# Reordering the first layer norm and the split of the feed-forward weights, signalling the selected rows in halves, and issuing fewer unread products, in a two-block transformer kernel on one core

## The reference

```python
logits = (h @ router_w + router_b)
top_v, top_i = lax.top_k(logits, TOP_K)            # 4 of 32
gates = jax.nn.softmax(top_v, axis=-1)
hid = xb @ w1[e] + b1[e]                           # rows chosen for expert e, 1024 -> 2048
y = clamped_swiglu(hid[:, :1024], hid[:, 1024:]) @ w2[e] + b2[e]
x = x + gf * segment_sum(y * gate)
x = rmsnorm(x, final_norm_w)                       # end of the first block
```

```python
h = layer_norm(2 ** 0.25 * x + mix @ w_out, ln1_g, ln1_b)
h = layer_norm(2 ** 0.25 * h + square(relu(h @ w_ff1)) @ w_ff2, ln2_g, ln2_b)
out = h + sigmoid(h @ w_ple_gate + b) * (p @ w_ple)
```

## Time and profile before

| | before |
|---|---|
| median of 3 runs (lowest, highest) | 1504.31 us (1504.18, 1506.39) |
| the profiled execution | 1501.75 us, span of the trace 1500.0 us |
| TensorE products busy | 1380.5 us (92%) |
| VectorE, ScalarE, GpSimd busy | 503.1, 311.3, 45.3 us |
| mean granted clock of TensorE | 0.981 |
| loaded | 500.01 MB, 333 GB/s over the span |

### The profile page before, as it was taken

The page is one execution under the profiler, slowest core; times in us unless marked ns, Lnnn a source line. Parts: engine busy times, 40 slices in busy tenths (PEclk is TensorE's granted clock), DMA queues, the critical chain, the costliest instruction groups (busy, mean ns, idle before and its releaser), DMA issues.

```text
span 1500.0 us, 17452 instructions
## 1 busy us (share of the span) xinstructions
PE 1380.5 (92%) x6836; PEld 747.5 (50%) x6836; DVE 503.1 (34%) x898; ACT 311.3 (21%) x454; POOL 45.3 (3%) x70
## 2 busy tenths in 40 slices
PE   5998999999989899999898998998999899899998
PEld 2884456433434324334333343243343487789987
DVE  2846435113113112121131131121111546755566
ACT  3515233101101101001011011010010453444451
POOL 2000002100000000000000000000000111000000
PEclk9999999999999999999999999999999999999999
DMA  9319906999999999999999999999999762465640
GB/s 388 117 52 368 415 4 221 412 428 428 428 428 430 428 429 429 429 428 429 429 428 428 430 428 429 428 429 428 429 429 428 320 224 74 153 184 182 195 141 29
DMA packets 61898, 500.01 MB, mean 333 GB/s; under 512 B 5192, under 2 KB 21864, under 8 KB 34144
## 3 DMA queue, kind: packets, MB, share of 16 engines
q1 hardware_dynamic: 59616, 492.85, 79.8%
q0 software_dynamic: 2032, 6.05, 1.3%
q10 hardware_dynamic: 208, 0.54, 0.1%
HBM read 498.37 MB, written 1.05 MB: 333 GB/s over the span
## 4 chain that ended last, share of the span: by engine, by line
PE 65%; DMA 22%; DVE 7%; issue 3%; ACT 1%; SPq 1%; DVEq 0%; ACTq 0%; PEldq 0%
PE bank L1553 27%; DMA ring<-in_w 20%; PE bank L635 17%; PE bank L673 15%; PE bank L693 2%; DMA ring<-in_w_in 2%; DVE dk L748 1%; DVE mrows L752 1%; DVE dk L742 1%; PE bank L681 1%; PE bank L655 1%; SPq L539 1%; PE bank L646 1%; SPq L592 0%; PE bank L1740 0%
## 5 line engine op out<-in xcount | busy, mean ns | idle before, releaser
L635 PE MATMUL bank<-ring,xn 128*64 128x512 f32 x2048 | 467.6, 610 | 66.2 <-DMA ring<-in_w 64.7
L635 PEld LDWEIGHTS bank<-ring,xn 128*64 128x64 f32 x2048 | 163.5, 140 | 360.2 <-issue 360.2
L673 PE MATMUL bank<-ring,dq 128*64 128x512 f32 x1024 | 226.8, 595 | 0.0
L737 DVE TENSOR_SCALAR mrows<-bank 128x512 f32<-128x512 f32 x32 | 20.6, 686 | 477.5 <-PE bank L635 477.5
L707 ACT ACTIVATE sq<-mrows 128x512 f32<-128x512 f32 x32 | 19.6, 630 | 774.5 <-DVE mrows L737 774.5
L673 PEld LDWEIGHTS bank<-ring,dq 128*64 128x64 f32 x1024 | 70.6, 137 | 136.5 <-issue 133.8
L761 DVE TENSOR_TENSOR dk<-bank,bc 128x512 f32<-128x512 f32 x32 | 22.1, 692 | 236.2 <-PE bank L673 236.2
L494 DVE TENSOR_TENSOR w_lo<-ring,w_hi 128x2048 fp32r<-128x2048 f32 x34 | 77.7, 2291 | 31.8 <-ACT w_hi L489 31.7
L1553 PE MATMUL bank<-x_hi,w_hi 128*128 128x256 f32 x256 | 73.2, 286 | 1.8 <-DVE h_lo L1434 1.8
L1553 PE MATMUL bank<-h_lo,w_hi 128*128 128x256 f32 x256 | 73.1, 285 | 0.0
L1553 PE MATMUL bank<-x_hi,w_lo 128*128 128x256 f32 x256 | 73.1, 285 | 0.0
(11 more groups left out here) (413 smaller groups left out, 1516.1 us busy)
## 6 DMA issues: line engine op xcount, KB each, us to landing
ring<-in_w SPq DMA_DIRECT2D x192, 2048.0 KB, 17.1
ring<-in_w_ff SPq DMA_DIRECT2D x32, 1024.0 KB, 5.5
ring<-in_w_ada SPq DMA_DIRECT2D x24, 1024.0 KB, 16.6
ring<-in_w_out SPq DMA_DIRECT2D x8, 1024.0 KB, 10.2
ring<-in_w_in SPq DMA_DIRECT2D x8, 992.0 KB, 25.2
ring<-in_w_in SPq DMA_DIRECT2D x8, 640.0 KB, 11.3
ring<-in_w_ple_gate SPq DMA_DIRECT2D x4, 1024.0 KB, 4.8
xc<-in_ctx SPq DMA_DIRECT2D x1, 1024.0 KB, 5.0
```

The costliest lines, as they stand in the source:

```text
L635: m = pe.matmul(banks[bank_no][mine(i), :], gathered[:, k, mine(i)], rows_of(at + i, 2)[:, k % 2, q * 512:(q + 1) * 512], start=k == 0, st ...
L673: m = pe.matmul(banks[OUT_BANKS[c]][mine(i), :], actT[:, k, mine(i)], rows_of(8 + 2 * j + i, 4)[:, r, c * 512:(c + 1) * 512], start=k == 0 ...
L737: dve.tensor_scalar(gs[:, half * 512:half * 512 + 512], banks[GATE_BANKS[half]][:], LIMIT, None, ALU.min)\
```

## The change

It does four things. In the diff the lines that begin with @@ name the function or the engine's program.

- `gather` signals `xt_full` after each half (k = 3 and k = 7), `gather_out` waits for and signals each half, and `hidden` waits for the first half at k = 0 and for the second at k = 4. The other waits count in halves.
- The two `keep_running` around the rank products have 1 and 2 products instead of 3 and 4.
- In the final norm of the first block ScalarE takes the root of tile 0 ahead of the squares of tile 1.
- Around the first layer norm: the first feed-forward chunk is rounded and subtracted ahead of the norm of tile 0; VectorE norms tile 1 directly behind tile 0 and takes the four low parts of `h1T` behind both; ScalarE takes root 1 ahead of the copies of the embedding banks, of which the last stands behind the roundings of tile 1; TensorE has the transposes of tile 1 ahead of the fourth embedding bank, and claims the banks of the sums behind `wide_part(0)`.

```diff
@@ gather, hidden
-            m.then_inc(moe("xt_full", which), 1)
+                if k % 4 == 3:
+                    m.then_inc(moe("xt_full", which), 1)
 
         def hidden(pe, n, which):
 
-            pe.wait_ge(moe("xt_read", which), n + 1)
             for k in range(KD):
                 at = k // 2 * 2
+                if k % 4 == 0:
+                    pe.wait_ge(moe("xt_read", which), n * 2 + (k // 4 + 1))
...
@@ pe_rest
-            pe.wait_ge(moe("xt_read", which), n + (1 + ahead))
+            pe.wait_ge(moe("xt_read", which), n * 2 + (2 + 2 * ahead))
...
@@ gather_out
-            act.wait_ge(moe("xt_full", which), n + 1)
             for j in range(2):
-                m = act.activation(gathered[:, 4 * j:4 * j + 4, :],
-                                   banks[GATHER_BANKS[j]][:].rearrange("p (k s) -> p k s", k=4), ACT.Copy)
-            m.then_inc(moe("xt_read", which), 1)
+                act.wait_ge(moe("xt_full", which), n * 2 + (j + 1))
+                act.activation(gathered[:, 4 * j:4 * j + 4, :],
+                               banks[GATHER_BANKS[j]][:].rearrange("p (k s) -> p k s", k=4), ACT.Copy)\
+                    .then_inc(moe("xt_read", which), 1)
...
@@ scalar: final norm of the first block
             for t in range(NT):
                 act.wait_ge(moe("y_added", MAIN), 4 * PAIRS - 1 + 2 * t)
                 step(act.activation(xn[:, 1, :], x2[:, t, :], ACT.Square, accum_out=stat[:, t:t + 1]), "ss3_done")
-            for t in range(NT):
                 act.wait_ge(sem("ms_done"), 6 + t)
                 step(act.activation(stat[:, 4 + t:5 + t], stat[:, 2 + t:3 + t], ACT.Sqrt), "root_done")
...
@@ scalar: first layer norm
             rounded("oT1", x_hi[:, 6:8, :])
+            round_weights(act, FIRST_FF)
+            def embedded(n):
+
+                t, c = divmod(n, 2)
+                name = f"ple{t}_{c}"
+                step(act.activation(ple[:, t, c * 512:(c + 1) * 512], take(act, name)[:], ACT.Copy), tile=name)
+
             for t in range(NT):
                 act.wait_ge(sem("ms_done"), 8 + t)
                 step(act.activation(stat[:, 16 + t:17 + t], stat[:, 12 + t:13 + t], ACT.Sqrt), "root_done")
+                for n in range(3 * t):
+                    embedded(n)
                 for j in range(2):
                     rounded(f"h1T{t}_{j}", x_hi[:, 4 * j:4 * j + 4, t * P:(t + 1) * P], 4)
-                if t == 0:
-                    round_weights(act, FIRST_FF)
-                    for n in range(4):
-                        t_, c = divmod(n, 2)
-                        name = f"ple{t_}_{c}"
-                        step(act.activation(ple[:, t_, c * 512:(c + 1) * 512], take(act, name)[:], ACT.Copy), tile=name)
+            embedded(3)
             for n in (FIRST_FF + 1, FIRST_FF + 2):
                 round_weights(act, n)
...
@@ vector: experts, first layer norm
-                dve.wait_ge(moe("xt_full", MAIN), pair + 1)
+                dve.wait_ge(moe("xt_full", MAIN), pair * 2 + 2)
...
             rest_of("oT1", x_lo[:, 6:8, :], x_hi[:, 6:8, :])
+            rest_of_weights(dve, FIRST_FF)
...
-            for t in range(NT):
-                layer_norm(t, "wo2", 12, 8, ln1g, ln1b, "h1_done")
+            layer_norm(0, "wo2", 12, 8, ln1g, ln1b, "h1_done")
+            layer_norm(1, "wo2", 12, 8, ln1g, ln1b, "h1_done")
+            for t in range(NT):
                 for j in range(2):
                     of = (slice(None), slice(4 * j, 4 * j + 4), slice(t * P, (t + 1) * P))
                     rest_of(f"h1T{t}_{j}", h_lo[of], x_hi[of], 4)
-                rest_of_weights(dve, FIRST_FF + t)
-            rest_of_weights(dve, FIRST_FF + 2)
+            for n in (FIRST_FF + 1, FIRST_FF + 2):
+                rest_of_weights(dve, n)
...
@@ tensor: ranks, embedding products, feed-forward
-            keep_running(bank("hfT1_3"), 3)
+            keep_running(bank("hfT1_3"), 1)
...
-            keep_running(bank("hfT1_3"), 4)
+            keep_running(bank("hfT1_3"), 2)
...
             for t in range(NT):
                 for c in range(2):
+                    if (t, c) == (1, 1):
+                        turn_one("h1T", x2, "h1_done", 1)
                     b = claim(pe, f"ple{t}_{c}")
...
-            turn_one("h1T", x2, "h1_done", 1)
-
-            sums = {(t, c): claim(pe, f"wide{t}_{c}") for t in range(NT) for c in range(2)}
...
             wide_part(0)
+            sums = {(t, c): claim(pe, f"wide{t}_{c}") for t in range(NT) for c in range(2)}
```

## The result

| | before | the change |
|---|---|---|
| median (lowest, highest), 4 runs each in turn | 1504.24 us (1501.37, 1506.39) | 1494.62 us (1493.45, 1495.66) |
| ratio, 95% interval | | 0.9944 [0.9931, 0.9958] |
| the profiled execution, its span | 1501.75 us, 1500.0 us | 1493.45 us, 1491.7 us |
| TensorE products; VectorE, ScalarE, GpSimd busy | 1380.5; 503.1, 311.3, 45.3 us | 1377.5; 503.7, 312.8, 45.2 us |

The account below looks back on a forecast made before the run. Full weight loads were taken to bound the expert stage, one engine at a time the stretches around it. Terms 1.7 + 1.1 + 5.6 + 1.5 = 9.9 us off 1504.31 gave 1494.4 us; 8-in-10 range 1490.5 to 1498.5.

Parts of the forecast that it names:

- Start: Start of the experts: first expert product 1.7 us earlier, bounds -1.5 and 2.4, from ranks, halved gather and clock together.
- (a) ranks earlier: Ahead of the gather: fewer unread products let the rank products start sooner, 0.9 us, at most 1.0.
- (b) gather in halves: Gather to first expert product: copying the first half during the second lets products follow directly, 1.4 us.
- (c) clock: Gather: TensorE at half clock until about 250 takes back 0.6 us; bounds 0 and 3.8.
- The start reaches the end: Expert stage: the 1.7 us gained at its start arrives undiminished, since the load stream is full from its first issue.
- The rival that the loads set the end by something else: Expert stage: loads set its end by something other than first issue, so the start gains nothing; 1496.1 us, chance 0.08.
- Inside the loop: Expert pairs: extra waits on TensorE and ScalarE cost 0, covered by TensorE's 4 us a pair of waiting for weights.
- Final norm: First block's final norm: tile 0's root before tile 1's squares moves scalings, transposes and next products 1.1 us; bounds 0, 1.3.
- Layer norm and feed-forward start: First layer norm: tile 1's norm directly behind tile 0's, remainders after both, gets the last remainder done 5.6 us earlier.
- Clock at the feed-forward: First feed-forward products: shorter TensorE waits avoid 3.3 us at half clock, worth 1.5 us, bounds 0 and 1.6.
- VectorE held before the norm: Ahead of tile 0's layer norm: VectorE waits for ScalarE's late rounding of feed-forward weights; 1508.3 us, slower, chance 0.03.
- the splits bind the feed-forward: Feed-forward: second weight chunk late by more than 1.8 us; a whole split late loses 4.2 us, 1498.6 us; chance 0.05.

Follow-up runs that it names:

- change_again: The change itself, unaltered, measured once more against the kernel before: 1494.62 us, ratio 0.9938.
- before_filled: The kernel before, plus 6 unread TensorE products behind the embedding products and 2 behind the last transposes ahead of the feed-forward: 1501.78 us, ratio 0.9992.
- unread_back: The change with 3 and 4 unread products around the rank products again, as in the kernel before: 1495.04 us, ratio 0.9948 to the kernel before.
- gather_whole: The change with one signal and one wait for both halves of the gather: 1495.45 us, ratio 0.9951 to the kernel before.
- split_behind: The change with VectorE subtracting the first feed-forward weights behind all four low parts, not ahead of the first norm: 1497.53 us, ratio 0.9966 to the kernel before.
- norm_undone: The change with its part around the first layer norm taken back on ScalarE, VectorE and TensorE: 1502.0 us, ratio 0.9996 to the kernel before.

## Why the prediction was right, and where it was not

The sum was 9.9 us, the trace has 8.3, and the ratio gives 8.4, within 6.3 to 10.4 (9.3 in `change_again`, within 7.2 to 11.4). In the trace the four stretches that the change touches give 9.74 us, and 1.44 went in the other three (0.57, 0.53 and 0.34 in the table). Part of the hit is luck: the base of 1504.31 us was the median of three runs, and in the later rounds the kernel before had 1502.27 to 1503.39, from which the same sum would give 1492.4 to 1493.5. By its steps:

- **Start, (a) ranks earlier, 0.9.** Measured 0.85 (ranks read 1.66 us after the sums, for 2.51). But that holds for one fall of the clock: `before_filled`, with the same start as the kernel before, took 10.89 us to the first expert product for 9.76, and `unread_back` 2.8 more than the change, 1.5 of it ahead of the ranks. I had priced the filling at one clock, and its own duration depends on the clock. Depending on the execution, the whole start is worth 1.6 or 2.8 us in the traces.
- **(b) gather in halves, 1.4.** Held: 1.43 of wait gone, and back in `gather_whole`.
- **(c) clock, -0.6.** Measured -0.72 (4.53 for 3.81): the full clock came back at 250.9, 1.5 us into the gather at half clock. The Trainium skill (TensorE: Matmul & The Clock Gate, HAM oscillation) says that each return to full clock is paid anew, and the gather does pay it; it does not pay enough to use up what (a) and (b) gain.
- **The start reaches the end.** The first expert product came from 7.28 to 10.95 us after the sums over the fourteen executions, and first product to last expert sum always took 933.5 to 934.6. The rival that the loads set the end by something else falls. Inside the loop the two signals cost nothing that can be seen.
- **Final norm, 1.1. This step failed** as a term that always holds, though its trace difference, 1.12, looks like a hit. I wrote that the transposes and the first products "hang on" VectorE's scalings, and gave TensorE's own path no price. It is the limit in two ways.
  Tile 0's transposes don't hang on them: TensorE comes to them 2.80 to 3.11 us after the last expert sum in every kernel, when its branch is over, however early tile 0 is scaled.
  Tile 1's transposes and the first product do hang on them, but only where TensorE is the faster. Before, these transposes waited 0.39 us for tile 1's scaling, and the first product came 6.27 us after the last expert sum, 1.01 behind the end of these scalings; in the change's first profile it came after 5.12, 0.96 behind them. From there to the layer norm both took 69.4 us, so in this pair the gain stands ahead of the first product. The half clock, which the kernel before had from 1192.4 to 1195.8, can be at most 0.4 of it: VectorE's first low part was ready only at about 1194.9. The rest, 0.8 to 1.1 (an estimate from these rows), is the root's.
  At half clock it is gone, since sixteen transposes then last as long as VectorE's chain: the scalings still moved by 1.1, the first product by 0.1 (6.19 for 6.28), and the layer norm by nothing (76.44 and 76.45).
  Of the ten profiles with the early root six had their first product 5.96 to 6.41 us after the sum, four 5.07 to 5.47; the four with the late root had 6.08 to 6.29. So the 1.1 of the sum came true in this pair by the luck of the clock. No run had the late root at full clock throughout, and what the step is worth on the median isn't shown.
- **Layer norm and feed-forward start, 5.6.** Measured 5.48; `split_behind` gives back 2.14 of it by putting one split where VectorE is the limit. Some of the 5.48 is of the clock: with the old order the first product came after 22.94 (`before_filled`) and 23.1 us (`norm_undone`), for 23.41, so the order itself is worth 5.0 to 5.5.
- **Clock at the feed-forward, 1.5.** Measured 1.50, in `before_filled` 1.46.
- **VectorE held before the norm** (the slower rival). It did not occur: the split ended 0.61 us before the projection was there, the 0.6 predicted. A late rounding by ScalarE itself wasn't tried. Nor did the splits bind the feed-forward: it took 181.27 us, and 181.31 with the old order at full clock.

Still open: why the jump over the overflow rounds takes TensorE 4 us, and what the kernel would gain without it. No run moved or removed it.

## What to carry to other kernels

When work sits between two halves of a chain on one engine, look for the idle stretch of that engine just ahead and move the work there: 2.29 us of VectorE work moved into a gap was worth 2.14 us and the clock behind it. Before a term is given to an earlier result, compare the consumer's start with the producer's end; a consumer that starts 0.8 us after it was released was waiting for something else. Then look at its sequencer's branches, which take no engine time and stand in no timeline: here one jump of 4 us set the start of the transposes in every kernel. And profile the same kernel twice before a term of one microsecond is believed.

## What the runs showed of the hardware

- The granted clock is not a property of the kernel alone. The change, unaltered, had 1.00 in one execution and 0.57 in another over 1189 to 1197, at a price of 1.9 us, more than the 1.1 of the edit that I had priced there.
- Filling can be the delay. Unread products meant to hold the clock ran at half of it themselves, 3.76 us for 1.97, and the gather stood behind them.
- A branch can cost microseconds. The jump over the overflow rounds took TensorE's sequencer 3.93 to 4.27 us in the fourteen profiles; the branches of its expert loop took 0.08 to 0.26 us in the change's. Matrix products issued ahead of the jump ran beside it.
- TensorE being busy did not give it the full clock. In the stretch 244 to 251 it was busy 6.73 of 7.00 us at 0.51; just ahead had been the router's products of 32 columns and waits. One more unread product in that front changed nothing, two had the full clock there in the execution profiled.
